# Gated delta layer: two heads at a time on 64x64 tiles, woven between the k-steps of the dn_qkv and dn_z projections

## The chip, the cores and the metric

One Trainium2 chip, one of its cores. The metric is the device time of one execution of the program in microseconds, lower is better.

## What is computed

Three layers on a sequence of 512 tokens, width 1024: an even layer (forget-gated and latent attention, each followed by a convolutional feed-forward), an odd layer (differential attention), and last a gated delta layer with an MLP. The change is in the last one, and in one helper that the odd layer uses too. Its core, for 8 heads of 128 dimensions and 8 chunks of C = 64 tokens:

```python
gc = jnp.cumsum(g, axis=-1)                       # log decay, inside a chunk
decay = jnp.exp(jnp.where(causal, gc[..., :, None] - gc[..., None, :], -jnp.inf))
lower = jnp.where(strict, jnp.einsum('bhnid,bhnjd->bhnij', k_beta, k) * decay, 0.0)
rhs = jnp.concatenate([v * beta[..., None], k_beta * jnp.exp(gc)[..., None]], axis=-1)
sol = lax.linalg.triangular_solve(lower + eye, rhs, left_side=True, lower=True, unit_diagonal=True)
u, w = sol[..., :DV], sol[..., DV:]
attn = jnp.einsum('bhnid,bhnjd->bhnij', q, k) * decay
def step(state, inp):                             # 8 chunks, one after the other
    q_c, k_c, u_c, w_c, a_c, gl = inp
    v_new = u_c - w_c @ state
    o_c = q_c @ state + a_c @ v_new
    state = state * gl + k_c.T @ v_new
    return state, o_c
```

q, k and v come out of a projection (`dn_qkv`), a convolution over 4 tokens and a silu; q and k are normalized per head. Another projection (`dn_z`) gates the result, a third (`dn_out`) brings it back to width 1024.

## The kernel before, in words

**Weights and projections.** Weights come from HBM in units of 128x2048 floats (1 MB), one DMA each on the SP queue, into two buffers `raw[0]`, `raw[1]`. ScalarE rounds a unit to fp32r (`wH`, helper `hi`, L825), VectorE forms the rest (`wL = raw - wH`, helper `lo`, L1211). A projection tile (128 outputs x 512 tokens) is 8 k-steps of three fp32r matmuls (hi*hi, lo*hi, hi*lo: L300, L301, L302). A unit holds two tiles, so 16 k-steps, 48 matmuls. `tile_wait` keeps TensorE from writing a bank before it was evacuated (`evac`). All engines have one program each in a fixed order, tied by semaphores: `tick(name, event)` adds to one, `at(event)` is the value to wait for.

**First units.** At the head of ffn0, odd_q, ffn1 and dn_qkv the first two units are computed k by k as the normalized inputs come in (`first_two_units`), the third unit uses banks 4 and 5, and the fourth (unit 3) waits for the evacuation of tiles 2 and 3 out of banks 2 and 3 (odd_q, dn_qkv). On VectorE the split of a coming unit's weights (`lo_next`) is issued ahead of the evacuations of the current one; `stream_scaled` (L1286 to L1298) does this for odd_q, odd_k and dn_z, and the dn_qkv loop (L1559 to L1571) is written the same way.

**Gated delta layer**, in the order in which TensorE runs it:

1. `dn_qkv`: 12 units (q, then k, then v). Per unit VectorE does one `lo`, two evacuations (L1565) and six convolution taps (L1570); ScalarE one `hi`, the fourth tap and the silu into `qkv`. Then the 16 gate rows (`wba`, 24 matmuls) and four small transposes (L676).
2. `dn_z`: 4 units; after each, 16 fp32 matmuls with one column for the squared norms of q and k (`key_norms`, L684).
3. Preparation, two heads at a time on 128x128 tiles (two chunks on the diagonal of a tile), banks 0 to 3 for one head and 4 to 7 for the other: spreads of per-token scalars (L706), grams (L712, L717), transposes (L726, L727), the inverse of the unit lower triangle by 5 doubling rounds (L745, then L755 and L756; the masks and subtractions L1645, L1651, L1652 on VectorE lie between them), and u and w (L762, L763). While it runs, TensorE has no projection to do.
4. Scan, 8 chunks for all 8 heads: w @ S (L785), q @ S (L790), k.T @ v_new (L796), attn @ v_new (L800); VectorE forms v_new (L1662) and the state (L1669); ScalarE copies the output out and squares it; sums L773.
5. Norm, gate (`gated`, L464 spreads a per-token factor) and `dn_out`.

An fp32 matmul shows in the trace as two MATMUL records, an fp32 transpose or an fp32r matmul as one.

Of the kernel before, what the change touches and what calls it, by code (L numbers as in the profile page):

```python
# [151 lines left out]
def build(nc, dram, known):  # L152
    ctx = ExitStack()
    with ctx:
# [35 lines left out]
        sq_heads = sq[:].rearrange("p a (b n) -> p (a b) n", n=P)  # L190
        rinv = dg[:].rearrange("p t n -> p (t n)")

        def stage(items):
# [21 lines left out]
        qkv, zT, S, vN, dconst, wba, tok = stage([  # L215
            ("qkv", [P, 24, SEQ]), ("zT", [P, H, SEQ]), ("S", [P, H, P]), ("vN", [P, H, P]),
            ("dconst", [P, 9 * P]), ("wba", [P, P]), ("tok", [P, 16, 32])])
        wbaH, wbaL = sb("wbaH", [P, P], F32R), sb("wbaL", [P, P], F32R)
        rowsT, gl, zed = sb("rowsT", [P, P]), sb("gl", [P, H, 8]), sb("zed", [P, 4, 16])
        o_at = base + 4 * 8 * SEQ  # L220
        oH, oL = sb("oH", [P, KT, SEQ], F32R, o_at), sb("oL", [P, KT, SEQ], F32R, o_at + 4 * KT * SEQ)
        attnT = sb("attnT", [P, H, SEQ], F32, h_at)
        kdec = sb("kdec", [P, H, SEQ], F32, h_at + 4 * KT * SEQ)
# [24 lines left out]

        def looped(name, per):
            return NUNITS[name] // per  # L250
# [3 lines left out]

        def tmp(p):

            names = ["lt", "y", "x", "t1", "r", "e"]
            slots = [y[:, k, :] for k in range(KT)] + [sq[:, k, :] for k in range(2)] + [dg[:].rearrange("p t n -> p (t n)"), ss[:]]
            return {n: slots[6 * p + k] for k, n in enumerate(names)}

# [33 lines left out]
        def _(pe):  # L294
# [373 lines left out]
            stream2("dn_qkv", first="mix2")  # L668
            pe.wait_ge(*at("dn.wba"))
            for k in range(KT):  # L670
                c = slice(k * 16, k * 16 + 16)
                last = three(bank[5][0:16, :], (wbaH[:, c], wbaL[:, c]), (hH[:, k, :], hL[:, k, :]), k == 0, k == KT - 1)
            last.then_inc(*tick("dn_pe", "dn.ba_rows"))
            pe.wait_ge(*at("dn.ba_scaled"))
            for t in range(TT):
                last = nc.tensor.transpose(bank[4][:, 16 * t:16 * t + 16], vN[0:16, t, :], ident[0:16, 0:16])  # L676
            last.then_inc(*tick("dn_pe", "dn.ba"))

            def key_norms(i, s):

                for a in range(4):
                    pe.wait_ge(*at(f"dn.sq{s}.{a}", i))
                    for t in range(TT):
                        last = mm(bank[7][:, bass.ds(i * 32 + (16 * s + 4 * a + t), 1)],  # L684
                                  y[:, 4 + a, t * P:(t + 1) * P], ones[:, 0:1], start=True, stop=True)
                last.then_inc(*tick("sums_pe", f"dn.sum{s}"))
                if peeled(i) and s == 1:
                    pe.wait_ge(*at("dn.g"))
                    mm(bank[5][:, 0:32], dconst[:, 0:P], tok[:, 1, :], start=True, stop=True)
                    mm(bank[5][:, 32:64], dconst[:, P:2 * P], tok[:, 1, :], start=True, stop=True)\  # L690
                        .then_inc(*tick("dn_pe", "dn.gc"))
            stream2("dn_z", more=key_norms, peel=1)
            pe.wait_ge(evac, TILE0["dn_out"])
            pe.wait_ge(*at("dn.rowset"))
            nc.tensor.transpose(bank[4][0:96, 0:P], tok[:, 8:11, :].rearrange("p a b -> p (a b)"), ident)\
                .then_inc(*tick("dn_pe", "dn.rows_turned"))
            pe.wait_ge(*at("dn.rows"))
            for h0 in range(0, H, 2):
                pair = [(h0 + p, [bank[4 * p + b] for b in range(4)], tmp(p)) for p in range(2)]
                for h, b, m in pair:  # L700
                    if h >= 2:
                        pe.wait_ge(*at(f"dn.w{h - 2}"))
                    for kind in (0, 2):
                        for t in range(TT):
                            r = 32 * kind + 4 * h + t
                            last = mm(b[kind][:, t * P:(t + 1) * P], ident[0:96, r:r + 1].to_broadcast([96, P]),  # L706
                                      rowsT[0:96, :], start=True, stop=True)
                    last.then_inc(*tick("dn_pe", f"dn.spread{h}"))
                for h, b, m in pair:
                    for t in range(TT):  # L710
                        c = slice(t * P, (t + 1) * P)
                        mm(b[1][:, c], qkv[:, 8 + h, c], qkv[:, h, c], start=True, stop=True)  # L712
                for h, b, m in pair:
                    pe.wait_ge(*at(f"dn.qn{h}"))
                    for t in range(TT):
                        c = slice(t * P, (t + 1) * P)
                        last = mm(b[0][:, c], qkv[:, 8 + h, c], m["t1"][:, c], start=True, stop=True)  # L717
                    last.then_inc(*tick("dn_pe", f"dn.gram{h}"))

                def token_major(h, b):  # L720

                    pe.wait_ge(*at(f"dn.diff{h}"))
                    pe.wait_ge(*at(f"dn.e{h}"))
                    for t in range(TT):
                        c = slice(t * P, (t + 1) * P)
                        nc.tensor.transpose(b[3][:, c], qkv[:, 8 + h, c], ident)  # L726
                        last = nc.tensor.transpose(b[2][:, c], qkv[:, 16 + h, c], ident)  # L727
                    last.then_inc(*tick("dn_pe", f"dn.turned{h}"))
                token_major(*pair[0][:2])
                for s in range(1, 6):  # L730
                    for h, b, m in pair:
                        if s == 1:
                            pe.wait_ge(*at(f"dn.y{h}.0"))
                            for t in range(TT):
                                c = slice(t * P, (t + 1) * P)
                                last = nc.tensor.transpose(b[0][:, c], m["y"][:, c], ident)
                            last.then_inc(*tick("dn_pe", f"dn.xt{h}"))
                            if h == h0:
                                token_major(*pair[1][:2])
                        pe.wait_ge(*at(f"dn.x{h}.{s - 1}"))  # L740
                        if s == 1:
                            pe.wait_ge(*at(f"dn.attn{h}"))
                        for t in range(TT):
                            c = slice(t * P, (t + 1) * P)
                            last = mm(b[1][:, c], m["lt"][:, c], m["x"][:, c], start=True, stop=True)  # L745
                        last.then_inc(*tick("dn_pe", f"dn.lx{h}.{s}"))
                    for h, b, m in pair:
                        pe.wait_ge(*at(f"dn.t{h}.{s}"))
                        if s == 1:
                            pe.wait_ge(*at(f"dn.tok{h}"))  # L750
                            pe.wait_ge(*at(f"dn.values{h}"))
                        for t in range(TT):
                            c = slice(t * P, (t + 1) * P)
                            if s < 5:
                                mm(b[2][:, c], m["y"][:, c], m["t1"][:, c], start=True, stop=True)  # L755
                            last = mm(b[3][:, c], m["t1"][:, c], m["y"][:, c], start=True, stop=True)  # L756
                        last.then_inc(*tick("dn_pe", f"dn.xx{h}.{s}"))
                for h, b, m in pair:
                    pe.wait_ge(*at(f"dn.y{h}.5"))
                    for t in range(TT):  # L760
                        c = slice(t * P, (t + 1) * P)
                        mm(b[0][:, c], m["y"][:, c], qkv[:, 16 + h, c], start=True, stop=True)  # L762
                        last = mm(b[1][:, c], m["r"][:, c], m["y"][:, c], start=True, stop=True)  # L763
                    last.then_inc(*tick("dn_pe", f"dn.uw{h}"))
            pe.wait_ge(*at(f"dn.w{H - 2}"))
            pe.wait_ge(*at(f"dn.w{H - 1}"))
            pe.wait_ge(*at(f"dn.qdec{H - 1}"))

            def output_sums(t):

                pe.wait_ge(*at(f"gated.sq{t}"))
                for h in range(H):
                    last = mm(bank[7][:, 4 * h + t:4 * h + t + 1], sq_heads[:, h, :], ones[:, 0:1], start=True, stop=True)  # L773
                last.then_inc(*tick("sums_pe", f"gated.sum{t}"))
# [48 lines left out]
        def _(act):  # L823
# [336 lines left out]
            for n in range(8):  # L1160
# [3 lines left out]
                if n == 2:  # L1164
                    hi_early("dn_out")
# [684 lines left out]
```

## Time and profile before

| | |
|---|---|
| median of 3 runs | 2336.46 us (2332.24 to 2338.17) |
| the profiled execution: its own time | 2333.22 us |
| its span, first to last instruction | 2331.3 us |
| mean granted TensorE clock | 0.945 |
| TensorE busy | 2201.5 us, 94% |
| VectorE, ScalarE busy | 1218.9 us, 803.7 us |
| HBM | 164 MB moved, 70 GB/s on average |

The span is the time between the first and the last instruction; 1.9 us lie around it. Times within the trace count from the span's start. A "granted clock" of 1.00 is 2.4 GHz, 0.50 is 1.2 GHz; a stretch between has parts at either level. TensorE's records overlap, since matmuls are pipelined: the time that one costs is read from the distance of two starts, not from its duration.

### The profile page before, as it was taken

What the parts mean: (1) busy time and instruction counts of PE and PEld (TensorE: products, weight loads), DVE (VectorE), ACT (ScalarE), POOL (GpSimd) and SP (SyncE); (2) the same over time, 40 slices, a digit from 0 to 9 for tenths busy, and PEclk for the clock granted to TensorE, in tenths of its full rate; (3) what the DMA queues carried; (4) which work ended last, traced back from release to release, by engine and by line L of the source; (5) the groups of instructions that cost most, each with busy time, mean ns of one, the idle gap of its engine ahead of it and who ended that gap; (6) DMA issues with size and microseconds to landing.
All of it is one profiled execution on the core that took longest, in us unless ns stands there. A gap on an engine that the chain in (4) does not pass through costs nothing.

```text
span 2331.3 us, 28001 instructions
## 1 busy us (share of the span) xinstructions
PE 2201.5 (94%) x10835; PEld 1818.8 (78%) x10835; DVE 1218.9 (52%) x1843; ACT 803.7 (34%) x1185; POOL 46.3 (2%) x30
## 2 busy tenths in 40 slices
PE   7989789999998997899999998999899999999998
PEld 6865577888887794678888886878888998888887
DVE  5345527643656337557534557762666335642542
ACT  4244534333334116444333334453211113321322
POOL 1000000000000001000000000000100000000000
PEclk9979999999999997899999998998999769999999
DMA  4101022223222220022223232221000002232221
GB/s 166 65 29 37 19 72 73 90 95 104 90 81 105 91 91 2 17 73 83 89 100 106 79 104 102 72 90 55 1 1 1 19 1 73 90 99 100 90 93 70
DMA packets 24722, 164.12 MB, mean 70 GB/s; under 512 B 2736, under 2 KB 2864, under 8 KB 8368
## 3 DMA queue, kind: packets, MB, share of 16 engines
q1 hardware_dynamic: 24048, 161.29, 20.4%
q8 instruction: 69, 1.13, 0.2%
q10 hardware_dynamic: 576, 1.46, 0.2%
q14 instruction: 29, 0.24, 0.0%
HBM read 160.65 MB, written 2.10 MB: 70 GB/s over the span
## 4 chain that ended last, share of the span: by engine, by line
PE 90%; DVE 6%; ACT 3%; issue 1%; DMA 0%; SPq 0%; ACTq 0%; DVEq 0%
PE bank L300 23%; PE bank L302 23%; PE bank L301 23%; PE bank L488 2%; PE bank L756 2%; PE bank L745 2%; PE bank L502 2%; PE bank L464 2%; PE bank L755 1%; PE bank L512 1%; PE bank L785 1%; PE bank L796 1%; PE bank L790 1%; PE bank L516 1%; PE bank L800 1%
## 5 line engine op out<-in xcount | busy, mean ns | idle before, releaser
L300 PE MATMUL bank<-hH,wH 128*128 128x512 f32 x1584 | 629.6, 398 | 26.6 <-DVE hL L1249 12.8
L302 PE MATMUL bank<-hH,wL 128*128 128x512 f32 x1584 | 624.7, 394 | 0.0
L301 PE MATMUL bank<-hL,wH 128*128 128x512 f32 x1584 | 624.6, 394 | 0.0
L1211 DVE TENSOR_TENSOR wL<-raw,wH 128x2048 fp32r<-128x2048 f32 x160 | 366.4, 2290 | 237.8 <-ACT wH L825 237.8
L825 ACT ACTIVATE wH<-raw 128x2048 fp32r<-128x2048 f32 x160 | 305.0, 1906 | 208.5 <-PE bank L302 204.7
L300 PEld LDWEIGHTS bank<-hH,wH 128*128 128x128 f32 x1584 | 303.2, 191 | 93.5 <-issue 15.8
L302 PEld LDWEIGHTS bank<-hH,wL 128*128 128x128 f32 x1584 | 302.2, 191 | 64.2
L301 PEld LDWEIGHTS bank<-hL,wH 128*128 128x128 f32 x1584 | 303.1, 191 | 62.8
L302 PE MATMUL bank<-mH,wL 128*128 128x512 f32 x608 | 236.6, 389 | 0.0
L301 PE MATMUL bank<-mL,wH 128*128 128x512 f32 x608 | 236.6, 389 | 0.0
L300 PE MATMUL bank<-mH,wH 128*128 128x512 f32 x608 | 236.5, 389 | 0.0
L300 PEld LDWEIGHTS bank<-mH,wH 128*128 128x128 f32 x608 | 114.1, 188 | 23.9
L302 PEld LDWEIGHTS bank<-mH,wL 128*128 128x128 f32 x608 | 114.1, 188 | 23.7
L301 PEld LDWEIGHTS bank<-mL,wH 128*128 128x128 f32 x608 | 114.1, 188 | 23.6
L825 ACT ACTIVATE y<-bank 128x512 f32<-128x512 f32 (+4 forms) x136 | 62.2, 480 | 118.7 <-PE bank L302 89.0
L825 ACT ACTIVATE qkv<-bank 128x512 f32<-128x512 f32 x24 | 13.5, 595 | 202.2 <-PE bank L763 119.4
L1494 DVE TENSOR_TENSOR ft<-bank,dg 128x512 f32<-128x512 f32 x44 | 30.4, 690 | 89.1 <-PE bank L302 89.0
L1318 DVE TENSOR_TENSOR ss<-ss,sq 128x512 f32<-128x512 f32 x48 | 33.3, 693 | 71.6 <-ACT sq L825 71.6
L1312 DVE TENSOR_TENSOR x<-x,bank 128x512 f32<-128x512 f32 (+1 forms) x24 | 16.5, 687 | 100.0 <-PE bank L302 99.9
L825 ACT ACTIVATE ft<-ft 128x512 f32<-128x512 f32 x44 | 27.8, 632 | 116.0 <-DVE ft L1499 116.0
L825 ACT ACTIVATE ft<-ft,vec 128x512 f32<-128x512 f32 x44 | 35.9, 815 | 85.7 <-DVE ft L1494 85.7
L825 ACT ACTIVATE mH<-y 128x512 f32 (+1 forms) x32 | 20.2, 632 | 120.9 <-DVE y L1695 120.9
(293 smaller groups left out, 2824.7 us busy)
## 6 DMA issues: line engine op xcount, KB each, us to landing
raw<-in_ffn_up SPq DMA_DIRECT2D x44, 1024.0 KB, 4.9
raw<-in_mlp_up SPq DMA_DIRECT2D x16, 1024.0 KB, 4.9
raw<-in_mlp_down SPq DMA_DIRECT2D x16, 1024.0 KB, 4.9
raw<-in_ffn_down SPq DMA_DIRECT2D x16, 768.0 KB, 4.3
raw<-in_dn_qkv SPq DMA_DIRECT2D x12, 1024.0 KB, 4.9
raw<-in_ffn_down SPq DMA_DIRECT2D x16, 640.0 KB, 3.9
raw<-in_even_in SPq DMA_DIRECT2D x9, 1024.0 KB, 4.9
raw<-in_even_out SPq DMA_DIRECT2D x4, 1024.0 KB, 4.9
```

The costliest lines, as they stand in the source:

```text
L300: mm(out, a, c, start=first, stop=False)
L301: mm(out, a, d, start=False, stop=False)
L302: return mm(out, b, c, start=False, stop=last)
L464: last = mm(bank[b][:, t * P:(t + 1) * P], stat[:, col + t:col + t + 1].to_broadcast([P, P]), ident, start=True, stop=True)
L488: last = mm(b[e][:, 0:n], q(u, e)[:, i * P:n], k(u, e)[:, 0:n], start=True, stop=not masked)
L502: last = nc.tensor.transpose(bank[4 + ti % 2][:, j * P:(j + 1) * P], ptile(buf, u, e, i)[:, j * P:(j + 1) * P], ident)
L745: last = mm(b[1][:, c], m["lt"][:, c], m["x"][:, c], start=True, stop=True)
L756: last = mm(b[3][:, c], m["t1"][:, c], m["y"][:, c], start=True, stop=True)
L825: return nc.scalar.activation(out, in_, func, **kw)
L1211: tt(wL[s][:], raw[s][:], wH[s][:].bitcast(F32), ALU.subtract).then_inc(w_split, 1)
L1318: tt(ss[:], ss[:], sq[:, a_ % 2, :], ALU.add).then_inc(*tick("sums_dve", f"{tag}.ss"))
L1494: tt(gate, bank[b0][:], rinv, ALU.mult).then_inc(evac, 1)
```

## The change

The heads are taken in 4 pairs. A tensor of a pair has head 2p on partitions 0 to 63 and head 2p+1 on partitions 64 to 127 (`part(a)`), and 8 chunks of 64 columns (`chunk(n)`). Where before four 128x128 matmuls served one head, now sixteen matmuls of 64-column tiles serve two heads.

The weight units of `dn_qkv` are reordered to k, q, v of pair 0, then of pair 1, and so on. Units 0 to 2 run as before, with the gate rows (`wba`) now inside unit 2. From unit 3 on, TensorE's program is written out slot by slot: window w (1 to 3) has the 48 k-steps of three dn_qkv units, window 4 the 64 k-steps of the four dn_z units, and ahead of each k-step it may issue a piece of the gates, of the preparation of pair w-1, and of a scan. VectorE and ScalarE follow the same slots.

```diff
+        def scan_slots(w):
+            if w < 2:
+                return []
+            if w < 4:
+                return [(w - 2, n, f, 6 * n + 2 * f) for n in range(8) for f in range(3)]
+            return ([(2, n, f, 5 * n + 2 * f) for n in range(8) for f in range(3)]
+                    + [(3, n, f, 40 + 3 * n + f) for n in range(8) for f in range(3)])
 ...
+            def small(b, left, right, event):
+                for n in range(8):
+                    for a in range(2):
+                        last = mm(bank[b][part(a), chunk(n)], left[part(a), chunk(n)], right(a, n), start=True, stop=True)
 ...
+            def to_tokens(p, f, heads, event):
+                for n in range(4):
+                    for a in range(2):
+                        last = mm(bank[4][part(a), n * P:(n + 1) * P], heads[2 * p + a][:, chunk(4 * f + n)], ident, start=True, stop=True)
 ...
+            def prep(p, t):
+                if t == 0: ...       # 16 matmuls of 64x64 (spread) and one 512-column fp32r matmul
+                if t == 1:
+                    grams(p, 3, kHead, f"dn.kk{p}")
+                if t == 2: ...       # beta spread, 16 matmuls
+                if t == 4:
+                    pe.wait_ge(*at(f"dn.din{p}"))
+                    grams(p, 2, qHead, f"dn.qk{p}")
+                if t == 6:
+                    pe.wait_ge(*at(f"dn.lt{p}"))
+                    spread_decay(p, 0)
+                if t == 7:
+                    pe.wait_ge(*at(f"dn.y{p}.0"))
+                    small(3, yp, lambda a, n: eye[part(a), :], f"dn.xt{p}")
+                if t == 8: ...       # spread_decay(p, 1)
+                if t == 10: ...      # column_sums, 8 matmuls of one column
+                for rnd in range(1, 6):
+                    if t == 4 + 6 * rnd:
+                        pe.wait_ge(*at(f"dn.x{p}.{rnd - 1}"))
+                        small(2, lt, lambda a, n: xT[part(a), chunk(n)], f"dn.lx{p}.{rnd}")
+                    if t == 7 + 6 * rnd:
+                        pe.wait_ge(*at(f"dn.t{p}.{rnd}"))
+                        if rnd < 5:
+                            small(2, yp, lambda a, n: dec[part(a), chunk(n)], None)
+                        small(3, dec, lambda a, n: yp[part(a), chunk(n)], f"dn.xx{p}.{rnd}")
+                # t = 12, 15, 18, 21: to_tokens for v and k
+            def scan(p, n, f):
+                if f == 0:           # waits scan.state{p}.{n-1} and the output's copy
+                    for a in range(2):
+                        mm(bank[5][part(a), 0:P], kHead[2 * p + a][:, chunk(n)], S[:, 2 * p + a, :], start=True, stop=True)
+                    for a in range(2):
+                        last = mm(bank[6 + a][:, 0:64], S[:, 2 * p + a, :], qHead[2 * p + a][:, chunk(n)], start=True, stop=False)
+                if f == 1:           # waits scan.r (VectorE)
+                    for a in range(2):
+                        last = mm(bank[5][part(a), P:2 * P], yp[part(a), chunk(n)], R[part(a), :], start=True, stop=True)
+                if f == 2:           # waits scan.vn (ScalarE)
+                    for a in range(2):
+                        mm(bank[6 + a][:, 0:64], vNew[part(a), :], ap[part(a), chunk(n)], start=False, stop=True)
+                    for a in range(2):
+                        last = mm(bank[6 + a][:, P:2 * P], kt[part(a), n, :], vDec[part(a), :], start=True, stop=True)
+            for w in range(1, 5):
+                for t in range(48 if w < 4 else 64):
+                    for p, n, f, at_slot in scan_slots(w):
+                        if at_slot == t:
+                            scan(p, n, f)
+                    if w == 1:
+                        gates(t)     # t = 0 waits dn.ba_scaled
+ ...
+                    prep(w - 1, t - turn(w - 1))      # turn is 9 for pair 0, else 0
+ ...
+                        dense("dn_qkv", 3 * w + t // 16, t % 16 // 8, t % 8)
+                    else:
+                        dense("dn_z", t // 16, t % 16 // 8, t % 8)
```

On VectorE, units 0 to 2 and the head of window 1; and in `stream_scaled`, where odd_q has `early=4`:

```diff
+            for u in range(3):
+                for tl in range(2):
+                    evicted(2 * u + tl)
+                if u == 0:
+                    lo_early("dn_qkv", 3)
+                taps((2 * u, 2 * u + 1))
             dve.wait_ge(*at("dn.ba_rows"))
+            tt(rows16[:], bank[7][0:16, :], rinv[0:16, :], ALU.mult).then_inc(*tick("dn_gate_dve", "dn.ba_scaled"))
 ...
                     for s in range(2):
-                        lo_next(name, i, s, early=early)
+                        if not early:
+                            lo_next(name, i, s)
                         for tl in range(2):
 ...
                             stt(dst(i, c), bank[bank_of(i, s, early) + tl][:].unsqueeze(1), scale, rinv.unsqueeze(1), ALU.mult, ALU.mult)\
                                 .then_inc(evac, 1)
+                        if early:
+                            lo_next(name, i, s, early=early)
```

Further: w is no longer formed in the preparation (the triangle's inverse is applied to R inside the scan, f = 1); decay and norm factors come from one exponent (`expo`) through Ln and Exp on ScalarE in place of roots and reciprocals; the convolution and z pieces of VectorE and ScalarE run inside the slots; the last `hi` and `lo` of dn_out's second unit come after the scan of pair 3. At the end of window 4 the squares, their sums (`column_sums`), the last z tile, the gated root and its reciprocal follow one another as before. No weight DMA is added or dropped; the DMAs of `dconst` and `wba` are issued earlier on ScalarE's queue.

## Rows read from the trace of the kernel before

**Rows 1.** The page: TensorE's busy time; the chain that ended last, by engine

```profile
PE 2201.5 (94%) x10835; PEld 1818.8 (78%) x10835; DVE 1218.9 (52%) x1843; ACT 803.7 (34%) x1185; POOL 46.3 (2%) x30
PE 90%; DVE 6%; ACT 3%; issue 1%; DMA 0%; SPq 0%; ACTq 0%; DVEq 0%
```

**Rows 2.** Busy time by stretch: stretch, length, PE, PEld, DVE, ACT, POOL; clock, DMA share, GB/s

```profile
1453.00:1559.00 106.00, 105.69 (x456) 84.69 (x456) 77.13 (x97) 44.08 (x53) 0.00 (x0) 0.98 0.26 89
1559.00:1624.00 65.00, 64.40 (x307) 55.17 (x307) 16.05 (x19) 26.93 (x40) 0.00 (x0) 0.87 0.19 65
1624.00:1816.00 192.00, 174.28 (x1400) 165.28 (x1400) 124.81 (x249) 43.95 (x118) 11.80 (x8) 0.96 0.00 1
1816.00:1840.00 24.00, 22.93 (x194) 21.99 (x195) 10.57 (x30) 3.43 (x6) 2.35 (x1) 0.99 0.01 2
1840.00:1894.00 54.00, 54.00 (x243) 51.28 (x242) 14.37 (x33) 6.09 (x7) 4.69 (x2) 0.50 0.06 20
1894.00:1915.00 21.00, 18.16 (x143) 17.38 (x142) 6.45 (x22) 3.85 (x5) 2.34 (x1) 0.91 0.00 1
```

**Rows 3.** Waits of TensorE in 1624:1816: total, times, longest

```profile
PE bank L736 <- DVE y L1632: 10.0, 8, 1.9
```

**Rows 4.** Timeline, TensorE, at unit 3 of dn_qkv and of odd_q

```profile
1453.14 0.77 PE L300 MATMUL bank<-hH,wH 128*128 128x512 f32 x1 [5.02 <-DVE y L1565]
...
770.47 0.76 PE L300 MATMUL bank<-hH,wH 128*128 128x512 f32 x1 [5.02 <-DVE qO L1297]
```

**Rows 5.** Timeline, TensorE: two matmuls of a projection

```profile
1487.14 0.39 PE L300 MATMUL bank<-hH,wH 128*128 128x512 f32 x1
1487.37 0.39 PE L301 MATMUL bank<-hL,wH 128*128 128x512 f32 x1
```

**Rows 6.** Timeline, TensorE: fp32 grams of 128x128, four matmuls to a row

```profile
1774.34 1.06 PE L717 MATMUL bank<-y,qkv 128*128 128x128 f32 x8
1775.23 1.06 PE L717 MATMUL bank<-sq,qkv 128*128 128x128 f32 x8
```

**Rows 7.** Timeline, TensorE: scores on 64 and on 96 rows; values on 64 weight columns

```profile
916.53 1.77 PE L488 MATMUL bank<-kO,qO 64*128 64x384 f32 x8
...
265.30 3.27 PE L488 MATMUL bank<-kM,qM 96*128 96x384 f32 x8
...
262.99 2.38 PE L516 MATMUL bank<-y,vM 128*64 128x512 f32 x16
```

**Rows 8.** Timeline, TensorE: eight scan matmuls of 128 weight columns on 64 columns

```profile
1818.93 2.00 PE L790 MATMUL bank<-qkv,S 128*128 128x64 f32 x16
```

**Rows 9.** Timeline, TensorE: a 32-column matmul, then 128-column ones, woven into projections

```profile
219.74 0.50 PE L300 MATMUL bank<-cqH,wH 128*128 128x512 f32 x1
...
221.33 1.05 PE L609 MATMUL bank<-qM,rope 96*32 96x512 f32 x2
222.30 0.50 PE L300 MATMUL bank<-cqH,wH 128*128 128x512 f32 x1
...
1926.35 0.47 PE L300 MATMUL bank<-oH,wH 128*128 128x512 f32 x1
...
1928.62 0.47 PE L300 MATMUL bank<-oH,wH 128*128 128x512 f32 x1
```

**Rows 10.** Timeline, VectorE and ScalarE: weights split, a 128x512 evacuation, a table load

```profile
1495.40 2.29 DVE L1211 TENSOR_TENSOR wL<-raw,wH 128x2048 fp32r<-128x2048 f32 x1 [2.50 <-ACT wH L825]
1497.61 0.68 DVE L1565 TENSOR_TENSOR y<-bank,dg 128x512 f32<-128x512 f32 x1
...
1559.18 1.28 ACT L825 ACT_TABLE_LOAD   x1
```

**Rows 11.** Timeline, TensorE: the scan's last matmuls, then the first spread of the norm

```profile
1907.08 1.89 PE L800 MATMUL bank<-attnT,vN 64*128 64x64 f32 x16
...
1915.28 6.75 PE L464 MATMUL bank<-const,stat 128*128 128x128 f32 x32 [1.34 <-DVE stat L1679]
```

**Rows 12.** Transposes of 16 rows, L676: count, durations, first and last start

```profile
L676 PE MATMUL bank<-const,vN x4: 208/208/230, 1559.6 to 1559.8; 16*128 16x16 f32 x4
```

**Rows 13.** Busy time around the woven 32-column matmuls, columns as in rows 2

```profile
215.00:242.00 27.00, 26.87 (x91) 14.21 (x90) 22.44 (x28) 8.92 (x13) 3.59 (x1) 1.00 0.08 25
```

More of the change, by code:

```diff
@@ L665, in _ @@
             ffn(1)
[L668 to L676, printed above, removed]
@@ L692, in _ @@
-            stream2("dn_z", more=key_norms, peel=1)
-            pe.wait_ge(evac, TILE0["dn_out"])
[L694 to L764, printed above, removed]
@@ new lines, in key_scalars @@
+            def key_scalars(p, t):
+                if t == 30:
+                    pe.wait_ge(*at(f"dn.ksq{p}"))
+                    for n in range(8):
+                        for a in range(2):
+                            last = mm(bank[4][part(a), n:n + 1], sq[:, a, chunk(n)], ones[:, 0:1], start=True, stop=True)
+                    last.then_inc(*tick("dn_scalar_pe", f"dn.ksum{p}"))
+                if t == 36:
+                    pe.wait_ge(*at(f"dn.expo{p}"))
+                    nc.tensor.transpose(bank[4][0:8, 0:P], expo[:, p, 2, :], ident).then_inc(*tick("dn_scalar_pe", f"dn.beta_turned{p}"))
@@ new lines, in column_sums, with spread_decay @@
+            def column_sums(what, p):
+                pe.wait_ge(*at(f"dn.{what}q{p}"))
+                for a in range(2):
+                    for t in range(TT):
+                        last = mm(bank[4][:, 4 * a + t:4 * a + t + 1], sq[:, a, t * P:(t + 1) * P], ones[:, 0:1], start=True, stop=True)
+                last.then_inc(*tick("dn_scalar_pe", f"dn.{what}um{p}"))
+            def spread_decay(p, a, b=4):
+                for n in range(8):
+                    r = 32 + 8 * p + n
+                    last = mm(bank[b][:, chunk(n)], ident[0:64, r:r + 1].to_broadcast([64, P]), rowsG[0:64, part(a)],
+                              start=True, stop=True)
+                last.then_inc(*tick("dn_prep_pe", f"dn.decay{p}.{a}"))
@@ L1160, in _ @@
[L1160 to L1171 removed]
+            act.wait_ge(*at("in.wba"))
@@ L1172, in _ @@
+            squares_of("os", 3, qHead, "scan.o3.7", "dn.osum2")
+            evacuated("dn_z", 7)
+            a(zT[:, 7, :], zT[:, 7, :], ACT.Silu).then_inc(*tick("dn_z_act", "dn.silu_z7"))
+            hi_early("dn_out")
             act.wait_ge(*at("gated.sums_scaled"))
@@ L1811 @@
     w = a["dn_w_in_2"][0]
-    arrays["dn_qkv"], arrays["dn_z"] = units(w[:, :3072], 256), units(w[:, 3072:4096], 256)
+    order = [u for pair in range(4) for u in (4 + pair, pair, 8 + pair)]
+    arrays["dn_qkv"], arrays["dn_z"] = units(w[:, :3072], 256)[order], units(w[:, 3072:4096], 256)
     arrays["wba"] = units(w[:, 4096:], 16)[0]
```

738 lines of the change are left out of this document (455 added, 283 removed).

## The prediction

> **What bounds the kernel now.** I read the page first: TensorE is busy 94% of the span and 90% of the chain that ended last [rows 1]. So time is won only by giving TensorE less to do, or less to wait for. Then busy time by stretch, over what the change rebuilds: from unit 3 of dn_qkv (1453) to the norm's first spread (1915), 462 us [rows 2]. In 1453 to 1559 it streams projections. In 1559 to 1624 dn_z carries the one-column sums, and the clock averages 0.87. The preparation takes 192 us with TensorE busy for 174, and its waits are short: 10.0 us for VectorE's first inverse in eight pieces [rows 3]. So this is no stage of idle time to be filled; its matmuls have to get cheaper. The scan takes 99 us, 54 of them at 1.2 GHz although TensorE never pauses there [rows 2]. Last, TensorE waits 5.02 us for evacuations at unit 3 of dn_qkv, and the same 5.02 at unit 3 of odd_q [rows 4].
>
> **Prices.** A projection matmul starts each 0.2275 us (two starts are 0.23 apart) [rows 5], a k-step of three takes 0.68, a unit of 16 takes 10.9. Four fp32 128x128 matmuls take 0.89 [rows 6], so one takes 0.224.
>
> The decisive price is that of `small`, sixteen 64x64 matmuls, which no row of before shows. Matmuls on disjoint halves of the array do run together: the scores on 64 rows take 1.77 us for the same columns that take 3.27 on 96 rows, and eight values matmuls with 64 weight columns each (2560 columns in all) take 2.38, half of what one after the other would need by the 0.224 [rows 7]. With 128 weight columns and only 64 moving ones, a matmul still costs 0.24 (2.00 us for eight) [rows 8], so the weights' load bounds it, and one of 64 weight columns should cost half, 0.112. Sixteen in pairs: 8 x 0.112 = 0.9 us. One after the other: 1.8 us. I take 0.9, by the nearest rows, which show both halves at once for rows and for columns; 1.8 stays for the range.
>
> A change of shape costs too. In the rotary stretch one 32-column matmul sits between six projection matmuls, period 2.56 us; 6 x 0.2275 + 4 x 0.22 leaves 0.33 for the way there and back, 0.165 for each change. Full 128x128 matmuls woven in the same manner (period 2.27 = 1.365 + 4 x 0.224) pay nothing [rows 9]. Ends: 0 and 0.25 for each.
>
> **The woven part, step by step.** I count TensorE's pieces over the 208 slots of windows 1 to 4.
> - Projections: 13 units x 10.92 = 142.0 us.
> - Groups of sixteen, or eight of to_tokens: per pair t = 0, 1, 2, 4, 7 (5), rounds 5 + 4 + 5 (14), tokens 4, key sums 1, so 24; four pairs and one group of the gates, 97 x 0.9 = 87.3.
> - spread_decay, 8 x 1.8 = 14.4 (128 weight columns, [rows 8]); one-column sums, 7 x 1.8 = 12.6; small rest 2.4.
> - Scan: 32 x (0.224 x 4 + 0.449) = 43.0. Before it was 32 matmuls a chunk, now 40, most in pairs.
> - Changes of shape: 343 in slot order, x 0.165 = 56.6.
>
> Together 358 us. The old stages' busy time over the same 462 us was 439, of which some 30 are clock. So halving the matmuls pays, and the weaving gives part of it back as shape changes: removing idle time is not what it does.
>
> **Waits that come in.** Unit 2 now holds the 24 gate matmuls (5.5 us, moved out of 1553 to 1559), so it ends near 1453.5, where the 5.02 us wait ends now. There slot 0 waits for `ba_scaled`, which VectorE reaches only after tile 5's evacuation, its six taps (4 us) and the tap on ScalarE: about 6.7 us, so +7. This takes the old stall's place rather than removing it. The gates' chain behind it has two table loads of 1.28 on ScalarE [rows 10], against four k-steps.
>
> In the slots VectorE has evacuations, taps and a weight split of 2.29 us ahead of each step of the inverse. After lx the next TensorE step is three projection k-steps off (2.05 us) against one 0.68 operation of VectorE and the latencies, about 1.0; after xx against two, about 1.7; each plus whatever stands ahead in VectorE's queue [rows 10]. That is about 6 us a window, and in window 4 the last scan has one k-step (0.68) between steps that need up to 1.3, some 1.15 a chunk: 4 x 6 + 9 = 33. Bounds: 0, and 75 if each of the 150 woven slots waits half a microsecond. VectorE's whole load is about 194 us (rows 2: 0.73 of time in dn_qkv, 125 in the preparation, halved by two heads to an operation), so it doesn't become the bound. SP's loads are spread over 29 us a unit instead of 10.9 and late for nobody; POOL's gates now come per head, early, all but the last two.
>
> I add 12, an allowance of 3% of the stretch, for the gates' chain, waits for two semaphores and instruction supply, and 8 for dips to 1.2 GHz: the old stretch lost about 27 in the scan and 8 in dn_z that way.
>
> Tail: from the last scan matmul to the first spread it is 6.4 us now (1908.9 to 1915.3) [rows 11]. Then it holds state and output copies, squares, sums, z's silu with a table load, dn_out's hi (1.9) and lo (2.3), and the root with another load: 11, less the last k-step, so 10.
>
> Sum: 7 + 358 + 33 + 12 + 8 + 10 = 428 against 462. Gain 34.
>
> **odd_q.** With the evacuations ahead of the split, tiles 2 and 3 leave their banks before unit 3 starts, so the 5.02 us wait goes [rows 4]. Behind it some 7 us ran at 1.2 GHz, half of it lost: 3.4. Gain 8.4; bounds 5 and 8.4. What is late next is the split for odd_k's first unit, which has a whole unit of time.
>
> Total: 42. The profiled execution took 2333.2 (span 2331.3), so 2291; the median lies 3.2 above it: **2294 us**.
>
> **Rivals.**
> *Small matmuls don't get faster.* If 64x64 halves don't overlap, or records can't follow each other quickly enough, each of the 97 groups costs 1 us more, and the scan some 20 us. The trace has no run of sixteen records under 0.106 us each; the nearest is four 16-row transposes with three starts in 0.2 us, about 0.065 each [rows 12]. At that pace a group's 32 records take 2.1 us instead of 0.9: 97 x 1.2 = 116, if no instruction runs ahead of the array. Result 2294 + 116 = 2410. Against it: averaged over the slots 4336 records x 0.065 = 282 us, under the 358, so a queue that fills during the projections' k-steps hides most. Deciding point: 42 us, that is 1.3 us for a group. Chance 0.14.
> The Trainium skill, "TensorE: Matmul & The Clock Gate", section "Wait — 56ns, not 53.3ns?", states that without hardware decode each matmul costs about 62 ns of the sequencer; by it a group would take 2.0 us and the whole about 2400. No run here shows which decode is on.
>
> *The clock stays low in the weave.* The old scan was busy throughout and ran 54 of 99 us at 1.2 GHz [rows 2]. The same share of the woven 358 us of work would take 490 us; with the 30 us of waits that slower matmuls would hide, about +100: 2394. It decides from 84 us at 1.2 GHz on, place: window 4 and its last scan. Against it: the rotary stretch, woven in the same way and with the same kind of gaps, ran 27 us at 1.00 [rows 13]. Chance 0.14.
>
> *The waits are larger.* VectorE's order puts taps or a split ahead of most steps: 75 instead of 33, or more at the start and the tail; 2336 at 75, which is no change. Chance 0.12.
>
> **How the numbers follow.** Forecast 0.60, its own range 2255 to 2325. Below it: shape changes at nothing and waits at nothing give 2294 - 57 - 33 = 2204 together, too much for both at once, half of it 2249. The range goes up to 2385, which leaves out most of the first rival and the upper part of the second. A measurement of this kernel can tell about 0.3% (7 us) from no change. Faster: the forecast but 0.02, a third of the larger waits and some milder forms of the clock and pace cases, 0.66; same: 0.07; slower: 0.27.
>
> **What would show it.** In the profile after: a group of sixteen small matmuls in 0.9 us (right) or near 2 (first rival); about 0.33 us lost around each; clock 0.9 or more over the woven stretch; TensorE's waits on VectorE there of 30 to 40 us in total; a wait of 6 to 7 us ahead of the first gate matmuls; no wait at odd_q's unit 3; the norm's first spread near 1873. A stretch from unit 3 to that spread of over 462 us makes the forecast wrong.

## The result, and the profile after

The changed kernel takes **2256.53 us** (median of 4 runs, 2255.65 to 2258.01) against 2334.52 (4 runs, 2332.24 to 2338.17) beside it: ratio 0.9665, 95% interval 0.9648 to 0.9682, or 78 us faster. Forecast: 2294, that is 42 us faster. The profiled execution took 2255.65 us, span 2253.9, clock 0.962 (before 0.945).

The page of the changed kernel, TensorE's busy time and the chain by engine, as in [rows 1]:

```profile
PE 2139.4 (95%) x12503; PEld 1706.3 (76%) x12503; DVE 1172.4 (52%) x1812; ACT 803.7 (36%) x1170; POOL 35.3 (2%) x26
PE 91%; DVE 4%; ACT 3%; issue 1%; DMA 0%; SPq 0%; DVEq 0%; ACTq 0%
```

TensorE has 62 us less to do, though 1668 records more, and is still the bound. The stretch that [rows 2] covers is now these two (columns as there): first gate matmul to the last projection matmul, and from there on to the norm's first spread included.

```profile
1449.70:1829.50 379.80, 375.15 (x4365) 281.57 (x4365) 190.92 (x394) 118.08 (x194) 7.66 (x6) 0.97 0.11 37
1449.70:1838.10 388.40, 377.26 (x4381) 283.44 (x4381) 194.91 (x400) 124.55 (x201) 10.19 (x8) 0.97 0.11 37
```

TensorE idles 4.65 us in the first (379.80 less 375.15). Its waits from the gates to the spread (wait, releaser: us, times, longest), which answer to [rows 3]:

```profile
PE bank L756 <- DVE rows L1873: 5.6, 1, 5.6
PE bank L514 <- DVE stat L1916: 5.3, 1, 5.3
PE bank L896 <- DVE qkv L1863: 3.4, 11, 1.6
PE bank L785 <- ACT sq L961: 1.3, 1, 1.3
PE bank L774 <- ACT kTok L961: 0.7, 1, 0.7
```

The first is the start of the weave, the second and fourth are its tail; inside are 3.4 us at the scan's w @ S (L896) and about one more. The inverse, which cost 10.0 us of waits before, costs none.

The timeline of TensorE in window 2 shows how a piece is priced. L808 is `small`, L350 to L352 are a k-step, L903 is a scan step:

```profile
1601.48 1.15 PE L808 MATMUL bank<-yT,dec 64*64 64x64 f32 x32
1602.56 0.50 PE L350 MATMUL bank<-hH,wH 128*128 128x512 f32 x1
1602.89 0.39 PE L351 MATMUL bank<-hL,wH 128*128 128x512 f32 x1
1603.12 0.40 PE L352 MATMUL bank<-hH,wL 128*128 128x512 f32 x1
1603.45 0.44 PE L903 MATMUL bank<-R,yT 64*64 64x128 f32 x4
```

Sixteen matmuls (32 records) take 1.08 us until the k-step starts (1601.48 to 1602.56). Two groups in a row show what one costs without a change of shape:

```profile
1487.37 1.15 PE L808 MATMUL bank<-dec,yT 64*64 64x64 f32 x32
1488.36 1.10 PE L808 MATMUL bank<-yT,dec 64*64 64x64 f32 x32
1489.39 0.50 PE L350 MATMUL bank<-hH,wH 128*128 128x512 f32 x1
```

Both take 2.02, so the second adds 0.94 to the 1.08 of a single one, and 0.14 of the 1.08 is the change. The k-step takes 0.89 (1602.56 to 1603.45) where 0.68 is its work: its first matmul takes 0.33 instead of 0.23, which is the way back, and its last one 0.33, which is the way into the next piece. A visit so costs 0.10 + 0.14 + 0.10 = 0.34 us. Group and k-step take 1.97 together, and the forecast's terms give 0.9 + 0.68 + 0.33 = 1.91.

Start and tail, as in [rows 4] and [rows 11]:

```profile
1449.72 1.88 PE L756 MATMUL bank<-dconst,rows 16*64 16x8 f32 x32 [5.55 <-DVE rows L1873]
...
1829.27 0.40 PE L352 MATMUL bank<-hH,wL 128*128 128x512 f32 x1
1830.92 1.95 PE L785 MATMUL bank<-const,sq 128*128 128x1 f32 x16 [1.26 <-ACT sq L961]
1838.15 1.19 PE L514 MATMUL bank<-const,stat 128*128 128x128 f32 x4 [5.28 <-DVE stat L1916]
```

**Where the 77.4 us of the two spans are.** Unit 2's projections end at 1448.1 before (5.02 ahead of [rows 4]'s first row), and would end at 1438.65 now (1444.2 less the 5.5 us of gate matmuls that it holds): 9.45 us. Not all of it comes from odd_q. Here are the same two ScalarE operations, one some 30 us ahead of odd_q's wait and one 91 us behind it, in the kernel before, in the changed one, and in the kernel before with odd_q's edit alone (experiment 1):

```profile
737.18 0.73 ACT L825 ACTIVATE hH<-x,vec 128x512 fp32r<-128x512 f32 x1 [0.90 <-DVE x L1267]
861.73 1.92 ACT L825 ACTIVATE wH<-raw 128x2048 fp32r<-128x2048 f32 x1 [9.61 <-PE bank L302]
```

```profile
734.64 0.73 ACT L961 ACTIVATE hH<-x,vec 128x512 fp32r<-128x512 f32 x1 [0.90 <-DVE x L1432]
851.93 1.92 ACT L961 ACTIVATE wH<-raw 128x2048 fp32r<-128x2048 f32 x1 [9.61 <-PE bank L352]
```

```profile
741.68 0.72 ACT L825 ACTIVATE hH<-x,vec 128x512 fp32r<-128x512 f32 x1 [0.90 <-DVE x L1267]
858.72 1.92 ACT L825 ACTIVATE wH<-raw 128x2048 fp32r<-128x2048 f32 x1 [9.61 <-PE bank L302]
```

Between them lie 124.55, 117.29 and 117.04 us, so odd_q gives 7.3 us in the changed kernel and 7.5 alone. Another 2.5 us were there ahead of odd_q's wait (737.18 against 734.64), in a part that the change leaves alone: the first 300 us were at 1.2 GHz for 47.8 us now and for 54.6 before. Some 0.3 us went the other way behind odd_q. From unit 2's end to the first spread it was 467.2 us (to 1915.28, [rows 11]) and is 399.5 (to 1838.15): 67.7 gained. After the spread 416.0 and 415.7. Sum 77.4.

**What the 67.7 us are.** The two stretches, before and now:

```profile
1448.12:1915.28 467.16, 439.47 (x2739) 395.82 (x2738) 252.41 (x449) 130.24 (x226) 21.18 (x12) 0.90 0.10 32
1438.65:1838.15 399.50, 382.78 (x4406) 287.66 (x4405) 204.92 (x415) 129.19 (x208) 10.19 (x8) 0.96 0.10 36
```

TensorE's idle time fell from 27.7 to 16.7 us, that is 11.0. Outside its long waits, TensorE was at 1.2 GHz for 93.5 us before, 54.6 of them in the scan, and is for 21.8 now. If half of such time is lost, 36 us of the gain are the clock's, and its work at full speed fell from 393 to 372, by 21. If 0.41 is lost, as in a scan of experiment 5, they are 29 and 27. So more than a third of the gain is a higher clock. Why the woven stretch keeps the clock that the old scan lost is open.

### The profile page after: what moved, and what is told of

Read it like the earlier page. It is cut to its first block, busy times and chain, and to the rows that moved or that the text cites. A ratio compares the mean times of both kernels' runs of the same rounds, so it can differ in the third digit from the quotient of the medians.

```text
span 2253.9 us, 31126 instructions
## 1 busy us (share of the span) xinstructions
PE 2139.4 (95%) x12503; PEld 1706.3 (76%) x12503; DVE 1172.4 (52%) x1812; ACT 803.7 (36%) x1170; POOL 35.3 (2%) x26
## 3 DMA queue, kind: packets, MB, share of 16 engines
q1 hardware_dynamic: 24048, 161.29, 20.5%
## 4 chain that ended last, share of the span: by engine, by line
PE 91%; DVE 4%; ACT 3%; issue 1%; DMA 0%; SPq 0%; DVEq 0%; ACTq 0%
PE bank L350 25%; PE bank L352 24%; PE bank L351 24%; PE bank L808 3%; PE bank L538 2%; PE bank L552 2%; PE bank L514 2%; PE bank L562 1%; PE bank L566 1%; PE bank L898 1%; PE bank L816 1%; PE bank L792 1%; PE bank L896 1%; PE bank L785 1%; ACT y L961 1%
## 5 line engine op out<-in xcount | busy, mean ns | idle before, releaser
L350 PE MATMUL bank<-hH,wH 128*128 128x512 f32 x1584 | 642.2, 405 | 16.5 <-DVE hL L1414 12.8
L352 PE MATMUL bank<-hH,wL 128*128 128x512 f32 x1584 | 624.2, 394 | 0.0
L350 PEld LDWEIGHTS bank<-hH,wH 128*128 128x128 f32 x1584 | 301.5, 190 | 89.5 <-issue 22.0
L352 PEld LDWEIGHTS bank<-hH,wL 128*128 128x128 f32 x1584 | 301.1, 190 | 64.6
L352 PE MATMUL bank<-mH,wL 128*128 128x512 f32 x608 | 236.6, 389 | 0.0
L350 PE MATMUL bank<-mH,wH 128*128 128x512 f32 x608 | 236.6, 389 | 0.0
L352 PEld LDWEIGHTS bank<-mH,wL 128*128 128x128 f32 x608 | 114.2, 188 | 23.8
L350 PEld LDWEIGHTS bank<-mH,wH 128*128 128x128 f32 x608 | 114.2, 188 | 23.8
L961 ACT ACTIVATE y<-bank 128x512 f32<-128x512 f32 (+4 forms) x128 | 57.4, 472 | 110.4 <-PE bank L352 89.0
L350 PE MATMUL bank<-wH,hH 128*128 128x256 f32 x192 | 54.4, 283 | 0.4 <-DVE vF L1593 0.4
```

The lines of the kernel that those rows point to most:

```text
L350: mm(out, a, c, start=first, stop=False)
L352: return mm(out, b, c, start=False, stop=last)
L961: return nc.scalar.activation(out, in_, func, **kw)
```

## The experiments

Ratios are to the kernel before, on the same chip. "Stretch" below is the time from the first gate matmul to the norm's first spread, 388.4 us in the changed kernel. Time at 1.2 GHz is what the granted clock's record has within it: 26.6 us in the changed kernel (four dips of 3.4, and 8.2 and 4.8 us of one of 10.2 at either end), 21.8 of them before the last projection matmul's end.

**1. odd_q's order alone, in the kernel before.**

```diff
+                        if not early:
+                            lo_next(name, i, s)
                         for tl in range(2):
 ...
+                        if early:
+                            lo_next(name, i, s, early=early)
```

> The kernel before, with one edit: in odd_q the evacuations come ahead of the split of the next weights. Theory (the wait at unit 3 and the 1.2 GHz stretch behind it go, and nothing is late in their place): 9 us faster, ratio 0.996, and no 5.02 us wait at odd_q's unit 3; the remaining 68 us of the change's 77 then belong to the gated delta layer. Rival (the stall moves to the split or the next unit): 0 to 3 us.

2330.56 us (12 runs) against 2336.61 (18 runs), ratio 0.9979 (0.9967 to 0.9992). Stretch 740 to 877 of the kernel before, then of this one:

```profile
740.00:877.00 137.00, 130.84 (x760) 114.67 (x759) 55.87 (x79) 27.97 (x29) 4.92 (x2) 0.98 0.26 87
```

```profile
740.00:877.00 137.00, 134.05 (x787) 117.43 (x785) 62.94 (x94) 32.99 (x40) 5.93 (x3) 1.00 0.26 90
```

Wait and dip are gone, as expected, and in its own place the edit gives 7.5 us (124.55 to 117.04, above). The medians show 4.9 us (1 - 0.9979), with an interval of 1.9 to 7.7, short of the 9 expected. In the profiled executions the first 300 us, which the edit doesn't touch, were at 1.2 GHz for 61.4 us here and 54.6 in the kernel before: this part varies between executions by nearly as much as the edit brings.

**2. The halves one after the other.** Both loops of `small`, `grams`, beta's spread, the key sums and `to_tokens` swapped, so that the sixteen matmuls are the same and neighbours sit on the same half.

```diff
-                for n in range(8):
-                    for a in range(2):
+                for a in range(2):
+                    for n in range(8):
```

> The changed kernel, with the two loops of 93 of the 97 groups swapped, so that all matmuls of one half come before those of the other: same matmuls, same slots, same waits, no two on disjoint halves next to each other. Theory (the gain is the pairing on disjoint halves of the array): each group grows from 0.93 to 1.86 us, +86 us, so 2343, slower than before; the weave alone would give nothing. Rival (the weave hides the small matmuls' time or instruction supply bounds them anyway): under +25 us.

2360.13 us (4 runs), ratio 1.0104 (1.0083 to 1.0124): the weave without the overlap is slower than the kernel before. Its windows up to the last projection matmul, and from its timeline one group of grams (L800) at full clock with what follows it; below them the same group of the changed kernel:

```profile
1457.50:1933.00 475.50, 471.21 (x4365) 369.37 (x4365) 191.79 (x393) 118.03 (x194) 7.62 (x6) 0.89 0.09 30
...
1475.54 1.90 PE L800 MATMUL bank<-qkv 128*64 128x64 f32 x32
1477.37 0.50 PE L350 MATMUL bank<-hH,wH 128*128 128x512 f32 x1
```

```profile
1465.51 1.15 PE L800 MATMUL bank<-qkv 128*64 128x64 f32 x32
1466.59 0.50 PE L350 MATMUL bank<-hH,wH 128*128 128x512 f32 x1
```

Busy time rises by 96 us, idle time doesn't (4.3). A group takes 1.83 us instead of 1.08. Over the 93 groups, the shorter ones of `to_tokens` among them, that is 66 us, and the clock is at 1.2 GHz for 105.4 us of the stretch instead of 26.6, half of which is 39 more lost at most: 105, near the 96. So the change lives on the order in which neighbours sit on different halves, and without it, about a third of the loss is the clock's.

**3 and 4. Fewer changes of shape.** The pieces of 2 (then 8) slots first, then their k-steps together, which leaves 306 (227) changes of the 343.

```diff
-                    dense("dn_qkv", 3 * w + t // 16, t % 16 // 8, t % 8)
+                    if t % G == G - 1:
+                        for t1 in range(t - G + 1, t + 1):
+                            dense("dn_qkv", 3 * w + t1 // 16, t1 % 16 // 8, t1 % 8)
```

> The changed kernel with the woven pieces of two slots issued together, then two k-steps: 306 changes of shape instead of 343, the same matmuls. Theory (0.165 to 0.18 us for a change, and waits of VectorE that stay hidden, since 1.36 us of k-steps still cover an operation of 0.68): 3 to 7 us faster than the changed kernel. Rival (waits of 33 us lie just under the surface and come out): 5 to 20 us slower.

> The changed kernel with the woven pieces of eight slots issued together, then the eight k-steps of a tile: 227 changes of shape instead of 343. Theory (the fine weave is what hides the chain over VectorE and ScalarE: some 1.0 us after lx, 1.7 after xx, 2.9 a chunk of the scan): 21 us less of shape changes, 60 to 110 us more of waits, so 2295 to 2345, with the clock dipping too. Rival (the engines' chain is short enough even without cover): 2235 to 2256.

By two: 2268.38 us (5 runs), ratio 0.9701 (0.9684 to 0.9719), and not the 3 to 7 us faster that were expected. The whole time doesn't tell it from the changed kernel, whose second repeat below has 0.9699. The stretch does, by one profile: 393.1 us, 4.7 longer, although 37 changes fewer should save about 6. 31.3 us of it were at 1.2 GHz against 26.6, and the scan's waits grew:

```profile
PE bank L896 <- DVE qkv L1866: 6.9, 6, 1.6
PE bank L908 <- ACT vDec L964: 2.5, 4, 0.6
PE bank L903 <- DVE R L1856: 1.8, 4, 0.4
```

By eight: 2341.61 us (5 runs), ratio 1.0029 (1.0013 to 1.0044); all that the change had gained is lost. Windows, then waits:

```profile
1451.00:1912.00 461.00, 402.43 (x4358) 332.07 (x4359) 189.70 (x395) 120.16 (x197) 8.89 (x7) 0.83 0.09 31
```

```profile
PE bank L896 <- DVE qkv L1866: 21.7, 19, 2.5
PE bank L908 <- ACT vDec L964: 11.0, 17, 0.7
PE bank L903 <- DVE R L1856: 6.4, 10, 1.4
...
PE bank L808 <- DVE dec L1824: 5.3, 3, 2.3
```

The stretch grew by 81 us (469.6). 461.00 less 402.43 is 58.6 idle against 4.65: 54 of them. Busy time grew by the other 27, although 116 changes fewer should save 19: 159.0 us of the stretch ran at 1.2 GHz against 26.6. So the other engines' work is hidden because the pieces are spread over single k-steps. With the idle time came more time at 1.2 GHz.

**5. Start and tail.** In the first run both edits, then each alone beside a repeat of the changed kernel. The head's edit scales the gate rows ahead of the taps of tiles 4 and 5; the tail's puts the split of dn_out's unit 1 behind the root (`hi`, ScalarE) and behind the factor (`lo`, VectorE).

```diff
+                if u == 2:
+                    dve.wait_ge(*at("dn.ba_rows"))
+                    tt(rows16[:], bank[7][0:16, :], rinv[0:16, :], ALU.mult).then_inc(*tick("dn_gate_dve", "dn.ba_scaled"))
                 taps((2 * u, 2 * u + 1))
-            dve.wait_ge(*at("dn.ba_rows"))
-            tt(rows16[:], bank[7][0:16, :], rinv[0:16, :], ALU.mult).then_inc(*tick("dn_gate_dve", "dn.ba_scaled"))
 ...
             out_sums(3)
-            lo_early("dn_out")
 ...
             chain(tt(stat[:, 0:32], stat[:, 0:32], q_inv, ALU.mult), "norm_dve", "gated.factor")
+            lo_early("dn_out")
```

> The changed kernel with the two waits at the ends of the woven stretch shortened: VectorE scales the gate rows ahead of the taps of tiles 4 and 5, and dn_out's second hi and lo come after the root and the factor. Theory (both waits are orders on VectorE and ScalarE, not work): the 5.6 us ahead of the first gate matmuls fall to about 1.5 and the 10 us at 1.2 GHz behind them shrink; the tail falls from 8.7 to about 5: 8 to 10 us faster than the changed kernel. Rival (the taps or the split are late then): 0 to 3 us.

> The changed kernel with the split of dn_out's unit 1 (hi on ScalarE, lo on VectorE) put behind the root and the factor; the gates as in the changed kernel. Everything that this edit moves is issued after the last scan matmul, so if the 27 us at 1.2 GHz in the last scan of the run with both edits came from the edits, they came from the other one. Theory: the last scan keeps the clock (under 5 us at 1.2 GHz between 1780 and 1830), the wait ahead of the norm's first spread falls from 5.3 to about 2.4 us, the time from the last projection matmul to that spread from 8.65 to about 5.8, and the kernel is 3 us faster than the changed one: 2253.5, ratio to before 0.966. Rival (the fall of the clock belongs to the tail's edit, or comes at random in any run): 20 to 30 us at 1.2 GHz in the last scan, 2265 to 2275.

> The changed kernel with the scaling of the gate rows ahead of the taps of tiles 4 and 5 on VectorE; the tail as in the changed kernel. Theory, if the head's edit causes the fall of the clock: the wait at the first gate matmul about 1.4 us (from 5.55) and a new one of 3.7 at the key sums, so nothing gained there, and 20 to 30 us at 1.2 GHz near 1790 to 1820, time 2268 to 2276, ratio 0.972 to 0.975. Rival (the fall needs both edits, or comes at random): no such stretch, 2253 to 2258.

> The changed kernel once more, beside the others of this set on the same chip. Both theories: 2254 to 2264; the stretches before 300 us run between 48 and 65 us at 1.2 GHz from one execution to the next, which moves the total by up to 9 us whatever was edited, so the others are compared with this one by their own stretches too.

> The changed kernel once more, beside the two edits on the same chip. Expected 2255 to 2258 in most executions, ratio 0.967, its last scan at full clock but for single dips of 3.4 us, woven stretch 379 to 380 us. If the fall of the clock in the last scan came at random, it could show here too (27 us at 1.2 GHz, 2265 to 2275).

| | median, us | ratio (95%) | stretch, us | 1.2 GHz in it, us |
|---|---|---|---|---|
| both edits | 2272.5 | 0.9727 (0.9701 to 0.9752) | 400.1 | 53.2 |
| tail alone | 2259.28 | 0.9686 (0.9663 to 0.9709) | 385.6 | 23.8 |
| head alone | 2270.08 | 0.9734 (0.9711 to 0.9758) | 400.0 | 49.7 |
| changed kernel, repeat 1 | 2257.41 | 0.9671 (0.9651 to 0.9691) | 388.3 | 26.5 |
| changed kernel, repeat 2 | 2262.96 | 0.9699 (0.9675 to 0.9723) | 388.5 | 26.6 |

Five runs each; the first and fourth row were measured side by side, and so were the other three. Both edits together were expected to win 8 to 10 us and cost 15. The tail's edit does its work: the wait at the spread falls from 5.3 to 2.4 us and the stretch by 2.9 us (388.5 to 385.6), as expected; the whole kernel's time can't show it: 2259.28 stands beside 2262.96, but the two repeats' medians lie 5.5 us apart.

The head's edit moves its wait and does not remove it:

```profile
PE bank L774 <- ACT sq L961: 3.8, 1, 3.8
...
PE bank L756 <- DVE rows L1873: 1.4, 1, 1.4
```

The key sums wait for squares that come no earlier. The first gate matmul starts 4 us earlier, which lengthens the stretch by as much and brings nothing: the kernel reaches the scan of pair 3 at 1771.5 where the changed kernel does at 1772.3, and loses 8.4 us in it. Windows of that scan, changed kernel, then head alone, then 28 us of the run with both edits:

```profile
1772.30:1825.80 53.50, 50.63 (x424) 34.14 (x425) 21.43 (x59) 13.12 (x28) 3.84 (x3) 1.00 0.12 40
```

```profile
1771.50:1833.40 61.90, 59.35 (x424) 39.16 (x424) 21.35 (x59) 13.13 (x28) 3.83 (x3) 0.83 0.10 35
```

```profile
1791.00:1819.00 28.00, 27.49 (x105) 18.14 (x107) 4.83 (x20) 3.16 (x9) 1.27 (x1) 0.51 0.00 1
```

The same 424 records, no more waits, and a clock of 0.83 instead of 1.00: 20.5 us at 1.2 GHz for 8.4 lost, 0.41 of it. With both edits it is 27.3 us in one piece, with TensorE busy 27.49 of 28. It is in both profiled executions with the head's edit and in none of the four without it. The mean clock of the whole execution was 0.950 to 0.956 in all ten with this edit and 0.957 to 0.962 in the 19 of the changed kernel and of the tail's edit, so the head's edit brings the fall. Why a shift of 4 us at 1446 decides over the clock at 1790 stays open.

**6. More work for VectorE.** Three (then six) chained small operations on a spare tile in each of the 208 slots, 224 ns each.

```diff
+                    [chain(tt(spare[:], ident[:, 0:64], ones[:, 0:64], ALU.mult), "spare_dve", f"spare{w}.{t}.{_r}") for _r in range(3)]
                     if t % 8 == 0 and l >= 6:
```

> The changed kernel with three more small operations on VectorE in each of the 208 slots (a product of two constants into a spare tile, each waiting for the one before), some 0.6 us a slot, 125 us in all, on top of 191. Theory (the pieces' three k-steps of cover leave slack, which is why the waits were 4.5 us and not 33): under 25 us slower than the changed kernel. Rival (VectorE stands just under the point where each step comes late): 60 us and more.

> The same with six operations a slot, some 250 us more, so that VectorE has about 440 us to do in a stretch of 380. Both theories: VectorE becomes the bound, 60 us slower at least; by the theory of slack most of the loss comes in this step (over twice that of three operations), by the rival it grows in proportion.

Three: 2289.42 us (4 runs), ratio 0.9800 (0.9779 to 0.9822), +32 us for 133 more of VectorE's work. Six: 2432.57 us (4 runs), ratio 1.0411 (1.0387 to 1.0436), +175. Windows of three, then of six:

```profile
1451.00:1865.00 414.00, 388.22 (x4366) 290.65 (x4366) 323.84 (x1020) 119.72 (x197) 7.71 (x6) 0.94 0.10 35
```

```profile
1455.00:2000.00 545.00, 443.24 (x4336) 333.20 (x4336) 463.67 (x1624) 118.62 (x193) 7.89 (x6) 0.82 0.08 26
```

The cost lies between the two expectations for three (under 25, or 60 and more), nearer the lower one, and grows more than fivefold from three to six: VectorE's chains had slack in most slots, which the first dose mostly fills. Idle time in the windows is 25.8 us, then 101.8; the time at 1.2 GHz in the stretch is 55.6 us, then 205.2. So idle time and clock share both costs.

## Why the prediction was right, and by what it was short

The direction held, and of its reason the part that was priced: paired small matmuls at 0.94 us a group, with shape changes giving part of it back. The size was half: 34 forecast for the rebuilt stretch, 67.7 measured. The result lies 1.5 us above the lower end of the stated range, 2255. That end was argued from half of the shape changes and of the waits falling away; the changes stayed whole and the waits nearly vanished, so that the result is inside is partly luck. From the end of unit 2 (1444.2) to the first spread it is 394.0 us against a forecast of 428, by its own terms:

| term | forecast | measured | from |
|---|---|---|---|
| start wait | 7 | 5.55 | L756's wait |
| woven work | 358 | 364.2 | 375.15 less 10.9 for the clock |
| waits in the weave | 33 | 4.65 | idle time in 379.80 |
| allowance | 12 | 0 | nothing left for it |
| clock | 8 | 10.9 | half of 21.8 us at 1.2 GHz |
| tail | 10 | 8.65 | 1829.5 to 1838.15 |

- **Woven work** is 6 us from its sum. Prices: a small group and a k-step 1.97 us against 1.91, a group 0.94 against 0.9, a visit 0.34 against 0.33, both forecast from [rows 7, 9]. (2.56 less 1.365 and 0.88 is 0.315 and not 0.33, which over 343 changes is under 3 us.) Experiment 2 shows the pairing, and that without it the change is a loss.
- **The step that failed is the waits: 33 forecast, 4.65 measured.** It said that after lx "the next TensorE step is three projection k-steps off (2.05 us)" against some 1.0 of VectorE and latencies, each "plus whatever stands ahead in VectorE's queue", and then charged that queue at 6 us a window. Both sides of that were mis-sized. The cover, the time that TensorE's own work gives VectorE, is longer: the slots in between hold pieces too, and every visit costs its change of shape, so the woven stretch's 208 slots take 1.83 us each (379.8 / 208), not the 0.68 of a k-step. From the last record of one group of the inverse to the next group that needs VectorE's result, the trace has 4.1 us at the median of 36 steps and 2.4 at the least. And the queue hardly stood ahead: VectorE's result was there 0.96 us after the group at the median, within 1.4 in 29 of the 36 and after 2.45 at the latest. Where cover was little longer than forecast, 2.4 to 2.5 us in pair 0's last rounds, there was no wait either. This is the closest of the 36, where the result comes 0.05 us ahead of the group that reads it:

```profile
1504.81 1.15 PE L808 MATMUL bank<-ss,lt 64*64 64x64 f32 x32
1507.50 0.68 DVE L1821 TENSOR_TENSOR dec<-bank,dconst 128x512 f32<-128x512 f32 x1
1508.23 1.15 PE L808 MATMUL bank<-dec,yT 64*64 64x64 f32 x32
```

  The last scan, charged at 1.15 a chunk, waited 2.8 us at L896 in all. Experiment 6 confirms slack and shows its end; experiment 4 shows that it is tied to the spread over single k-steps.
- **The allowance of 12** was for nothing that the trace shows. It and the waits are 40 us too many, start and tail 3; woven work and clock, 9 too few, leave the 34 by which this stretch was forecast too long.
- **The clock of the old stretch** was read too high: the prediction has "some 30" of the 439 us of busy time as the clock's, but its own [rows 2] give 47, with 8 in the preparation and 4 elsewhere beside dn_z and the scan. The sum doesn't use it, but the account of where the gain comes from does: what "halving the matmuls pays" is 21 to 27 us, and the clock gives 29 to 36.
- **odd_q**: 8.4 forecast, 7.3 in its own place (7.5 alone; 4.9, with 1.9 to 7.7, in medians). The wait's 5.02 held. The clock's 3.4 was too much: the 6.8 us at 1.2 GHz lie at 767.7 to 774.5, so 2.8 of them pass while TensorE still waits, and the nine slow matmuls behind (770.47 to 774.44) cost 1.9.
- **Small matmuls don't get faster** (0.14): refuted. 32 records pass in 1.08 us, 0.034 each, against the 0.065 of [rows 12]. The Trainium skill, "TensorE: Matmul & The Clock Gate", section "Wait — 56ns, not 53.3ns?", names about 62 ns for each matmul without hardware decode; that rule doesn't describe this run, which is nearer the 25 ns that the same section gives as the least for narrow matmuls: 0.94 us for a second group in a row is 29 ns a record.
- **The clock stays low in the weave** (0.14): not here, 21.8 us against the 84 from which it decides. But its place was real: the scan of pair 3 is where the head's edit brought 20.5 us at 1.2 GHz, and 27.3 together with the tail's. Experiments 2, 4 and the six operations of 6 brought 105 to 205 us of it over the stretch.
- **The waits are larger** (0.12): they were smaller. Experiment 4 had 58.6 us idle, and with the clock that it lost came to 2341.61, near the 2336 that this rival gives for 75 us of waits.

What a tuner could still take is small: the tail's edit wins 2.9 us in its place, which the whole kernel's measurement doesn't tell apart; no version tried is shown to beat the changed kernel.

## What to carry to other kernels

Two heads of 64 on the two halves of the array nearly halve the cost of small fp32 matmuls (1.83 us to 1.08 for sixteen here), but only if the neighbours in the instruction order sit on different halves; look for that order first. When small pieces are woven between large ones, count as cover for a dependence the real length of the slots between, pieces and shape changes included, and not the large matmuls alone; then keep the pieces single: bunching them by eight saved shape changes and cost far more in waits and clock, and by two it gained nothing. Count the clock as well as the work when you explain a gain: here it was at least as large as what the cheaper matmuls gave. Removing a wait early in a stretch can be paid for in clock some 340 us later, as here: read the granted clock of the whole run after each such edit.

## What the runs showed of the hardware, unexpected

- **Unpaired small matmuls came with a lower clock.** With the same matmuls one half at a time TensorE is as busy (471.21 of 475.50) and is granted 0.89 instead of 0.97 (375.15 of 379.80).
- **A TensorE busy all the time may be granted 1.2 GHz**: 27.49 of 28 us busy at 0.51, in a stretch that at other executions' full clock holds the same matmuls.
- **A change of shape costs at both ends.** The matmul ahead of a small group and the one behind it take 0.33 us instead of 0.23, the group 1.08 instead of 0.94: 0.34 for the visit. The Trainium skill, "TensorEngine Tiling (Array Packing)", section "Key Properties", says that changing the tiling mode drains the engine and gives no time. The trace shows the 0.34 us, but not whether a drain is what takes them.
- **The first 300 us vary.** The changed kernel's three profiled executions spent 47.8, 51.2 and 64.9 us of them at 1.2 GHz, and took 2255.65, 2255.9 and 2264.62 us, all with a stretch of 388.3 to 388.5. A gain of under 5 us elsewhere has to be read in its own stretch.
